# Lo parts of queries and keys on GpSimd instead of VectorE, in a fused attention, pooling and feed-forward step

## The chip, the cores and the metric

The kernel runs on one core of a Trainium2 chip. The metric is device time in microseconds (us); the median of three runs before the change is 1396.32 us (1395.48 to 1396.6).

## The reference, cut to what matters

One transformer layer, in fp32, for a prompt of 1024 rows and for 8 decoding samples with 4096 cached rows each. The part around the change is the prompt's attention: 8 heads of 64 columns, causal, with a bias from summed log forget gates.

```python
def fox_prompt(q, k, v, logf):
    Fh = jnp.cumsum(logf, axis=1).transpose(0, 2, 1)
    ...
    s = einsum('bqhd,bkhd->bhqk', q_blk, k) * HEAD_DIM ** -0.5
    s = s + (F_blk[..., :, None] - Fh[..., None, :])
    s = where(kpos <= qpos, s, NEG_INF)
    p = softmax(s, axis=-1)
    return einsum('bhqk,bkhd->bqhd', p, v)
```

The rest of the layer: projections of prompt and samples, a pooling mixer, attention of the samples over their cached pages, the output product, two layer norms and a gated feed-forward product.

## The kernel before, in words

**Hi and lo parts.** A product in full fp32 is made as a sum of matmuls in a faster rounded type (fp32r). Each operand x is split into a hi part (x rounded, a copy, made by ScalarE) and a lo part (x - hi, a subtraction). For a weight tile the hi part is in `WH`, the lo part in `WL`; for the prompt's rows they are `XH` and `XL`. For the queries and keys of a pair of heads both parts of both heads lie in `R2`: six tiles of 128x1024, three per head. Tile 3*hh has the query (hi in the head's own 64 partitions, lo in the other 64), tiles 3*hh+1 and 3*hh+2 the key's hi part twice and its lo part twice, so that two matmuls of 128 contraction rows make all four terms. The raw query is in `QX` (ACC tile 6), the raw key in `KX[p % 2]` (ACC tiles 7 and 4).

**Slots.** The prompt's attention runs over four pairs of heads (p = 0 to 3) with 16 slots each (s = 0 to 15; slots 0 to 7 are head 0, 8 to 15 head 1); x = 16 * p + s counts them all, 64 in sum. Slot x makes one tile of 128 query rows against up to 1024 keys. In each slot the engines do this, each in an order written out by hand:

- TensorE: scores of x (L1264 and L1268, into `S`, PSUM banks 0 and 1), extra turns (transposes) in some slots, a first half of product steps, the turn of the probabilities of x-1 (L1218, into `TB`, PSUM banks 4 and 5), a second half of product steps, then the weighted values of x-2 (L1278, into `OB`). The product steps (L1205, three matmuls each) are shares of the projections for the next pair, dealt over the slots beforehand (`CHUNKS`): in slot 1 of a pair three and three for pairs 0 to 2, four and three for pair 3.
- VectorE: bias and row minimum of the scores (L1748), then what else the slot has, then the copy of turned probabilities out of `TB` for even x-1 (L1791), a reciprocal (L1795), and the scaling of the weighted values of x-2 (L1809).
- ScalarE: exponentials (L989), the copies of finished projections out of PSUM (`keep`, L892 to L895), the copy of turned probabilities for odd x-1 (L1008), hi parts.

`TB` is one tile that all turns share, in a fixed order (`T`). In slot 1 of every pair TensorE turns the raw values of that pair into `TB` right after the scores (L1218 again), VectorE copies them to `VN[p % 2]` (L1783), and only then may TensorE write the turn of the probabilities of the slot before into `TB` (`claim_tb` waits for `tb_free`).

**The lo parts of queries and keys** are made by VectorE, one instruction of 64x1024 each, counted by the semaphore `conv_lo`: `query_lo(p, hh)` (L1631) and `key_lo(p, hh, n)` (L1637, n = 0 and 1). Those of head 0 of pair p+1 come in slots 11 (query), 12 and 13 (keys); those of head 1 of pair p in slot 0 (query) and slot 1 (both keys), in each slot right behind L1748 and ahead of everything else, and so ahead of L1783 in slot 1. Those of pair 0 are made before slot 0. ScalarE makes the hi parts just ahead (`query_hi` L902 in slots 10 and 15, `key_hi` L909 in slots 11, 12 and 0; semaphore `conv_hi`). Who waits for `conv_lo`: the scores of the first tile of a head (slots 0 and 8), `keep` before it overwrites the raw query or key tile, and GpSimd at its pauses.

**GpSimd in these slots** subtracts the lo parts of later weight tiles (`entry_rest`, L778, ten in all, among them at slots 10, 16, 21, 26, 32, 37, 42 and 48) and multiplies pages of cached keys by the first two samples' queries (`multiply`, L769, 32 of them, two pages or 128x1024 each). The multiplications are spread over the slots of `EMUL`, none of them in slots 0, 1, 11, 12 or 13 of a pair:

```python
ESLOTS = [x for x in range(8, 48) if x % STEPS not in (0, 1, 11, 12, 13)]
EMUL = tuple(ESLOTS[n * len(ESLOTS) // EARLY] for n in range(EARLY))
ERED = tuple(x + 1 for x in EMUL)
```

VectorE reduces each product one slot later (`reduce_keys`, L1654, slots `ERED`), and SP loads the next pages behind the reductions. GpSimd isn't tied to the slots but by what it waits for; the two waits for `conv_lo` (its pauses), at s = 2 of pairs 1 and 2 and at s = 14 of pairs 0 and 1, keep its next multiplications behind VectorE's subtractions.

**Behind the prompt** come the mixer and the samples' projections (from about 320 us), the output product with the first layer norm (from about 400 us), and then the feed-forward product, into which the samples' attention over cached pages is woven.

Of the kernel before, what the change touches and what calls it, by code (L numbers as in the profile page):

```python
# [24 lines left out]
F32 = mybir.dt.float32  # L25
# [3 lines left out]
ALU = mybir.AluOpType  # L29
# [5 lines left out]
KC = D // P  # L35
# [6 lines left out]
PAIRS = H // 2  # L42
# [20 lines left out]
NWT = 3 * PAIRS + GROUPS  # L63
WS = 3
# [30 lines left out]
ENTRY = {n + WS: x for n, x in LASTSLOT.items() if n + WS < NWT}  # L95
# [43 lines left out]
EMUL = tuple(ESLOTS[n * len(ESLOTS) // EARLY] for n in range(EARLY))  # L139
# [71 lines left out]
def build(nc, t):  # L211
    ctx = ExitStack()
    with ctx:  # L213
# [520 lines left out]
        def _(pool):  # L734
# [21 lines left out]
            def multiply(n):  # L756
# [9 lines left out]
                if c == 0:  # L766
# [2 lines left out]
                pool.tensor_tensor(keys, keys, QB[:].rearrange("p (o n) -> p o n", o=1).to_broadcast([P, KP, AW]),  # L769
                                   ALU.mult).then_inc(k_mul, 1)  # L770

            def entry_rest(n):

                e = KC + n
                pool.wait_ge(ent_hi, e + 1)
                pool.wait_ge(ent_lo, e)
                hi, lo = WH[:, tile_slot(n), :], WL[:, tile_slot(n), :]
                pool.tensor_tensor(lo, WR[:, raw_slot(e), :], hi.bitcast(F32), ALU.subtract).then_inc(ent_lo, 1)  # L778

            for x, p, s in slots():  # L780
                if x == 6:
                    pool.wait_ge(tb_free, T["g", 1] + 1)
                    for b in range(NB):
                        pool.dma_start(G_d[b], GT[:, b // 4, (b % 4) * NPAGE * H:(b % 4 + 1) * NPAGE * H]).then_inc(g_st, 16)
                if s == 2 and 1 <= p < PAIRS - 1:
                    pool.wait_ge(conv_lo, 6 * p + 6)
                if s == 14 and p + 1 < PAIRS - 1:
                    pool.wait_ge(conv_lo, 6 * (p + 1) + 3)
                for n in range(2 * WS, NWT):
                    if ENTRY[n] + 1 == x:  # L790
                        entry_rest(n)
                for n in range(EARLY):
                    if EMUL[n] == x:
                        multiply(n)
# [821 lines left out]
        def _(dve):  # L1616
# [8 lines left out]
                    hi, lo = (part[:, max(0, e - 1), 0:ROWS] for part in (XH, XL))  # L1625
                dve.tensor_tensor(lo, WR[:, raw_slot(e), :], hi.bitcast(F32), ALU.subtract).then_inc(ent_lo, 1)  # L1626

            def query_lo(p, hh):
                a, b = slice(64 * hh, 64 * hh + 64), slice(64 - 64 * hh, 128 - 64 * hh)
                dve.wait_ge(conv_hi, 6 * p + 3 * hh + 1)  # L1630
                dve.tensor_tensor(R2[b, 3 * hh, :], QX[a, :], R2[a, 3 * hh, :].bitcast(F32), ALU.subtract  # L1631
                                  ).then_inc(conv_lo, 1)

            def key_lo(p, hh, n):
                a, b = slice(64 * hh, 64 * hh + 64), slice(64 - 64 * hh, 128 - 64 * hh)
                dve.wait_ge(conv_hi, 6 * p + 3 * hh + 2)
                dve.tensor_tensor(R2[(a, b)[n], 3 * hh + 2, :], KX[p % 2][a, :], R2[a, 3 * hh + 1, :].bitcast(F32),  # L1637
                                  ALU.subtract).then_inc(conv_lo, 1)

            def reduce_keys(n):  # L1640
# [73 lines left out]
            dve.scalar_tensor_tensor(out=fa, in0=fz, scalar=-1.0, in1=fz, op0=ALU.mult, op1=ALU.max).then_inc(f_z, 1)  # L1714
            dve.wait_ge(f_t, 1)
            dve.tensor_scalar(fnf, fb, 1.0, None, ALU.add).then_inc(f_u, 1)
            query_lo(0, 0)
            dve.wait_ge(f_l, 1)
            link(dve.tensor_scalar(fnf, fnf, -1.0, None, ALU.add))
            link(dve.tensor_tensor(fnf, fb, fnf, ALU.subtract))  # L1720
# [3 lines left out]
            dve.wait_ge(f_done, 1)  # L1724
            link(dve.tensor_tensor_scan(fnf[:, 0:ROWS], fone, fz[:, 0:ROWS], 0.0, ALU.mult, ALU.subtract))
            dve.tensor_scalar(fnf[:, 0:ROWS], fnf[:, 0:ROWS], 1.0 / SCALE, None, ALU.mult).then_inc(f_done, 1)
            key_lo(0, 0, 0)
            key_lo(0, 0, 1)
            dve.wait_ge(ob_full, O["ft"] + 1)
            dve.wait_ge(small_lo, 2)  # L1730
            link(dve.tensor_copy(f_rows.rearrange("p i h -> p (i h)"), OB[:, 0:RT * H]))
            dve.tensor_copy(f_new[:], OB[0:NB, RT * H:(RT + 1) * H]).then_inc(ob_free, 1)
            query_lo(0, 1)
            key_lo(0, 1, 0)
            key_lo(0, 1, 1)
            for n in range(WS):
                entry_lo(KC + WS + n)

            for x, p, s in slots():
                if x < SLOTS:  # L1740
                    hh, i = s // RT, s % RT
                    w = (i + 1) * P
                    dve.wait_ge(s_full, U["s", x] + 1)
                    if i == 0:
                        dve.wait_ge(nf_ld[hh], 16 * (p + 1))
                    if x >= 2:
                        dve.wait_ge(tb_full, T["t", x - 2] + 1)
                    dve.tensor_tensor_reduce(L[x % 2][:, 0:w], S[:, 0:w], NF[hh][:, 0:w], -SCALE, 3e38,  # L1748
                                             ALU.add, ALU.min, negm[:, x % 2:x % 2 + 1]).then_inc(s_free, 1)
                if s == 11 and p + 1 < PAIRS:  # L1750
                    query_lo(p + 1, 0)
                if s in (12, 13) and p + 1 < PAIRS:
                    key_lo(p + 1, 0, s - 12)
                if s == 0 and 1 <= p < PAIRS:
                    query_lo(p, 1)
                if s == 1 and 1 <= p < PAIRS:
                    key_lo(p, 1, 0)
                    key_lo(p, 1, 1)
                for n in range(EARLY):
                    if ERED[n] == x and EMUL.index(EMUL[n]) == n:  # L1760
                        reduce_keys(n)
                if x in (3, 5):
                    m = (x - 3) // 2
                    dve.wait_ge(ob_full, O["q", m] + 1)
                    dve.tensor_copy(QB[0:NB, 2 * m * P:(2 * m + 2) * P], OB[0:NB, 0:2 * P]).then_inc(ob_free, 1)
                if x == 2:
                    dve.wait_ge(suf_scan, 2)
                    dve.wait_ge(ob_full, O["c"] + 1)
                    for m in range(2):
                        ls = LS[:, m, :].rearrange("p (h k) -> p h k", h=H)  # L1770
                        tot = OB[:, m * H:(m + 1) * H].rearrange("p (h o) -> p h o", o=1).to_broadcast([P, H, P])
                        ins = dve.tensor_tensor(ls, tot, ls, ALU.subtract)
                    ins.then_inc(ob_free, 1)
                if x in (4, 5):
                    m = x - 4
                    dve.wait_ge(tb_full, T["g", m] + 1)
                    dve.tensor_copy(GT[:, m, :].rearrange("p (r h) -> p r h", h=H),
                                    TB.rearrange("p (h r) -> p r h", h=H)).then_inc(tb_free, 1)
                if s == 1 and p < PAIRS:
                    dve.wait_ge(tb_full, T["vn", p] + 1)  # L1780
                    if p >= 2:
                        dve.wait_ge(vn_st, 16 * (p - 1))
                    dve.tensor_copy(VN[p % 2], TB).then_inc(tb_free, 1)  # L1783
                v = x - 1
                if 0 <= v < SLOTS:
                    if v % 2 == 0:
                        w = (v % RT + 1) * P
                        dve.wait_ge(tb_full, T["t", v] + 1)
                        if v >= 2:
                            dve.wait_ge(ob_full, O["pv", v - 2] + 1)  # L1790
                        dve.tensor_copy(PT[0][:, 0:w], TB[:, 0:w]).then_inc(tb_free, 1)  # L1791
                    dve.wait_ge(e_done, v + 1)
                    if v >= 2:
                        dve.wait_ge(ob_free, O["pv", v - 2] + 1)
                    dve.reciprocal(rinv[:, v % 2:v % 2 + 1], rsum[:, v % 2:v % 2 + 1]).then_inc(inv_done, 1)  # L1795
                for n in range(EARLY):
                    if ERED[n] == x and EMUL.index(EMUL[n]) != n:
                        reduce_keys(n)
                if x in MIXSLOT:
                    mixer_output(MIXSLOT[x])  # L1800
                v = x - 2
                if v >= 0:
                    q, r = divmod(v, STEPS)
                    hh, i = r // RT, r % RT
                    dve.wait_ge(ob_full, O["pv", v] + 1)
                    dve.wait_ge(inv_done, v + 1)
                    if r == 0 and q >= 1:
                        dve.wait_ge(tb_full, T["ct", q - 1] + 1)
                    dve.tensor_scalar(AO[:, i * P + hh * HD:i * P + hh * HD + HD], OB[:, 0:HD],  # L1809
                                      rinv[:, v % 2:v % 2 + 1], None, ALU.mult).then_inc(ob_free, 1)  # L1810
                if x < 2:
                    dve.wait_ge(logf_ld, 32)
                    dve.wait_ge(mask_done, 1)
                    link(dve.tensor_tensor_scan(LS[:, x, :], scanmask, LF[:, x, :], 0.0, ALU.mult, ALU.add))
                    dve.tensor_copy(suftot[:, x, :], LS[:, x, :].rearrange("p (h k) -> p h k", h=H)[:, :, P - 1]
                                    ).then_inc(suf_scan, 1)
                if x + 1 in MIXSLOT:
                    mixer_input(MIXSLOT[x + 1])
                if x == SLOTS - 2:
                    output_lo(0)  # L1820
# [451 lines left out]
```

## Time and profile before

| | us |
|---|---|
| median of three runs | 1396.32 |
| the profiled execution's own time | 1396.35 |
| its span, first to last instruction | 1394.5 |
| TensorE matmuls busy | 1343.7 (96%) |
| TensorE weight loads busy | 1078.8 (77%) |
| VectorE busy | 693.9 (50%) |
| ScalarE busy | 358.6 (26%) |
| GpSimd busy | 548.5 (39%) |
| mean granted TensorE clock | 0.989 |

How to read it: the engines run beside each other, each through its own list of instructions in order, and wait for each other by semaphores. Busy times add up over the whole span and say nothing of where an engine waits; the list of waits and the timeline do. PE is TensorE's matmuls, PEld its weight loads, DVE is VectorE, ACT ScalarE, POOL GpSimd. A granted clock of 1.00 is 2.4 GHz and of 0.5 is 1.2 GHz. Names left of the arrow are written, names right of it read; `AR` and `ACC` are large tiles of which `VN`, `L`, `PT`, `QX` and `KX` are parts, and R stands for `R2`.

### The profile page before, as it was taken

The numbers are of one execution on the slowest core, as the hardware profiler recorded it, in microseconds if no ns is written. First come the engines' busy times: TensorE is split into PE (matmuls) and PEld (weight loads), VectorE is DVE, ScalarE is ACT, GpSimd is POOL, SyncE is SP. The second block draws the span as 40 slices with busy tenths as digits, with TensorE's granted clock in tenths as the row PEclk, the third lists the DMA queues.
The fourth block names the chain that finished last, engine by engine and source line by source line (L and its number), as shares of the span: only waits on it lengthen the run. The fifth ranks groups of instructions, "written<-read, shape, count | busy, mean of one in ns | idle before, by whom it ended". The sixth has DMA issues, their size and how long they took to land. (4 is left out here: it accounts for less than half of the span.)

```text
span 1394.5 us, 21289 instructions
## 1 busy us (share of the span) xinstructions
PE 1343.7 (96%) x7605; PEld 1078.8 (77%) x7605; DVE 693.9 (50%) x1038; ACT 358.6 (26%) x527; POOL 548.5 (39%) x262
## 2 busy tenths in 40 slices
PE   7899999999989899999999999999999999999997
PEld 5889999999869886677777777777777776666675
DVE  4745665653556583553546465544634334321327
ACT  3524444443341233112021202121210201111116
POOL 1014454704110036656575657566562212121114
PEclk9999999999989999999999999999999999999999
DMA  7334453511035216777777777778776445367533
GB/s 246 104 116 150 129 185 103 170 43 53 25 107 219 86 45 220 256 243 243 231 261 240 243 247 241 234 236 266 222 253 215 158 141 202 152 262 277 223 145 122
DMA packets 111769, 255.02 MB, mean 183 GB/s; under 512 B 12848, under 2 KB 22961, under 8 KB 106280
## 3 DMA queue, kind: packets, MB, share of 16 engines
q1 hardware_dynamic: 102384, 247.00, 53.0%
q10 hardware_dynamic: 8320, 4.19, 1.1%
q0 software_dynamic: 960, 2.47, 0.5%
q8 instruction: 60, 0.98, 0.3%
q14 instruction: 45, 0.37, 0.1%
HBM read 243.73 MB, written 10.12 MB: 182 GB/s over the span
## 5 line engine op out<-in xcount | busy, mean ns | idle before, releaser
L829 POOL TENSOR_TENSOR WL<-WR,WH 128x1024 fp32r<-128x1024 f32 x55 | 132.1, 2402 | 427.4 <-ACT WH L1051 427.4
L769 POOL TENSOR_TENSOR AR<-AR,QB 128x1024 f32<-128x1024 f32 x96 | 232.6, 2439 | 101.1 <-DMA AR<-cache_k 88.5
L1454 PE MATMUL PSM<-XH,WH 128*128 128x512 f32 x672 | 215.7, 402 | 0.0
L1454 PE MATMUL PSM<-XL,WH 128*128 128x512 f32 x672 | 210.7, 395 | 0.0
L1454 PE MATMUL PSM<-XH,WL 128*128 128x512 f32 x672 | 210.7, 394 | 0.0
L2029 DVE TENSOR_TENSOR ACC<-ACC,PSM 128x512 f32<-128x512 f32 x160 | 108.7, 684 | 141.6 <-PE PSM L1464 141.5
L1454 PEld LDWEIGHTS PSM<-XH,WH 128*128 128x128 f32 x672 | 121.9, 188 | 53.3 <-issue 27.6
L1051 ACT CAST WH<-WR 128x1024 fp32r<-128x1024 f32 x55 | 57.5, 1047 | 367.3 <-PE PSM L1454 189.5
L1454 PEld LDWEIGHTS PSM<-XH,WL 128*128 128x128 f32 x672 | 126.3, 188 | 29.9
L1454 PEld LDWEIGHTS PSM<-XL,WH 128*128 128x128 f32 x672 | 126.2, 188 | 29.6
L1464 PE MATMUL PSM<-R 128*128 128x512 f32 x528 | 148.5, 390 | 0.1
L1654 DVE TENSOR_REDUCE AR<-AR 128x16 f32<-128x1024 f32 x80 | 96.8, 1211 | 91.5 <-POOL AR L769 91.5
L1464 PE MATMUL PSM<-WH,R 128*128 128x512 f32 x352 | 140.6, 400 | 0.1
L1205 PE MATMUL PSM<-XH,WH 128*128 128x344 f32 x384 | 134.2, 350 | 5.7 <-DVE WL L1626 4.7
L1205 PE MATMUL PSM<-XH,WL 128*128 128x344 f32 x384 | 123.7, 322 | 0.0
L1205 PE MATMUL PSM<-XL,WH 128*128 128x344 f32 x384 | 123.5, 322 | 0.0
L1464 PEld LDWEIGHTS PSM<-R 128*128 128x128 f32 x528 | 99.0, 188 | 22.1 <-DVE R L2017 0.5
L989 ACT ACTIVATE AR<-AR,negm 128x128 f32<-128x128 f32 (+3 forms) x64 | 49.7, 777 | 157.0 <-DVE negm L1748 157.0
L1464 PEld LDWEIGHTS PSM<-WH,R 128*128 128x128 f32 x352 | 66.1, 188 | 29.3 <-issue 12.8
L1205 PEld LDWEIGHTS PSM<-XH,WH 128*128 128x128 f32 x384 | 73.4, 191 | 8.8 <-DVE WL L1626 5.5
L2010 DVE TENSOR_TENSOR AR<-AR,PSM 128x1024 f32<-128x1024 f32 x21 | 25.6, 1220 | 107.9 <-PE PSM L1454 102.0
L1205 PEld LDWEIGHTS PSM<-XL,WH 128*128 128x128 f32 x384 | 73.4, 191 | 0.7 <-issue 0.7
(266 smaller groups left out, 2144.3 us busy)
## 6 DMA issues: line engine op xcount, KB each, us to landing
AR<-cache_v SPq DMA_DIRECT2D x256, 256.0 KB, 3.3
AR<-cache_k SPq DMA_DIRECT2D x192, 256.0 KB, 3.5
AR<-ws SPq DMA_DIRECT2D x37, 1024.0 KB, 6.4
WR<-ffn SPq DMA_DIRECT2D x66, 512.0 KB, 4.8
WR<-w_in SPq DMA_DIRECT2D x20, 512.0 KB, 4.7
ACC<-cache_k SPq DMA_DIRECT2D x32, 256.0 KB, 3.0
WR<-cache_k SPq DMA_DIRECT2D x32, 256.0 KB, 3.0
WR<-w_o SPq DMA_DIRECT2D x5, 1024.0 KB, 4.9
```

The lines of the kernel that those rows point to most:

```text
L769: pool.tensor_tensor(keys, keys, QB[:].rearrange("p (o n) -> p o n", o=1).to_broadcast([P, KP, AW]), ALU.mult).then_inc(k_mul, 1)
L829: pool.tensor_tensor(lo, WR[:, raw_weight(e), :], hi.bitcast(F32), ALU.subtract).then_inc(ffn_lo, 1)
L989: act.activation(L[x % 2][:, 0:w], L[x % 2][:, 0:w], ACT.Exp, scale=-1.0, bias=negm[:, x % 2:x % 2 + 1], accum_out=rsum[:, x % 2:x % 2 + 1 ...
L1051: act.copy(weight_slot(kind, f)[0], WR[:, raw_weight(e), :]).then_inc(ffn_hi, 1)
L1205: ins = pe.matmul(third(n, m), w[a][:, tile_slot(n), k * P:(k + 1) * P], x[b][:, k, m * TH:(m + 1) * TH], start=(k == 0 and (a, b) == PART ...
L1454: ins = pe.matmul(out[:, hc], (hi, lo)[a][:, k * P:(k + 1) * P], x[b][:, k, hc], start=(k == 0 and n == 0), stop=(k == KC - 1 and n == 2))
L1464: ins = pe.matmul(PSM[:, 2 + n % 4, :], R2[:, 2 * r + a, i * P:(i + 1) * P], w[b][:, half * HALF:(half + 1) * HALF], start=(r == 0 and m = ...
L1654: dve.tensor_reduce(out[:, c * KP:(c + 1) * KP, :].rearrange("p j h -> p (j h)"), keys.rearrange("p (a n) -> p a n", n=HD), AX.X, ALU.add) ...
L2010: dve.tensor_tensor(GU, GU, PSM[:, 2:4, :].rearrange("p a n -> p (a n)"), ALU.mult).then_inc(gu_done, 1)
L2029: dve.tensor_tensor(cols, cols, PSM[:, 2 + n % 4, :], ALU.add).then_inc(d_free, 1)
```

## The change

The lo parts of pairs 1 to 3 are made by GpSimd, in the same slots as before (11, 12, 13, 0 and 1), each behind a wait for `conv_hi` and followed by a wait for its own `conv_lo`. Ahead of each group GpSimd waits until its own multiplications (`k_mul`) and weight subtractions (`ent_lo`) of earlier slots have finished. The two pauses at s = 2 and s = 14 are gone. In slots with an `entry_rest` (16, 32, 48) the query's subtraction stands ahead of it. Pair 0's lo parts stay on VectorE, at the same places.

```diff
@@ gpsimd
+            def query_lo(p, hh):
+                a, b = slice(64 * hh, 64 * hh + 64), slice(64 - 64 * hh, 128 - 64 * hh)
+                pool.wait_ge(conv_hi, 6 * p + 3 * hh + 1)
+                pool.tensor_tensor(R2[b, 3 * hh, :], QX[a, :], R2[a, 3 * hh, :].bitcast(F32), ALU.subtract
+                                  ).then_inc(conv_lo, 1)
+                pool.wait_ge(conv_lo, 6 * p + 3 * hh + 1)
+
+            def key_lo(p, hh, n):
+                a, b = slice(64 * hh, 64 * hh + 64), slice(64 - 64 * hh, 128 - 64 * hh)
+                pool.wait_ge(conv_hi, 6 * p + 3 * hh + 2)
+                pool.tensor_tensor(R2[(a, b)[n], 3 * hh + 2, :], KX[p % 2][a, :], R2[a, 3 * hh + 1, :].bitcast(F32),
+                                  ALU.subtract).then_inc(conv_lo, 1)
+                pool.wait_ge(conv_lo, 6 * p + 3 * hh + 2 + n)
...
-                if s == 2 and 1 <= p < PAIRS - 1:
-                    pool.wait_ge(conv_lo, 6 * p + 6)
-                if s == 14 and p + 1 < PAIRS - 1:
-                    pool.wait_ge(conv_lo, 6 * (p + 1) + 3)
+                if s in (0, 1) and 1 <= p < PAIRS or s in (11, 12, 13) and p + 1 < PAIRS:
+                    pool.wait_ge(k_mul, sum(at < x for at in EMUL))
+                    pool.wait_ge(ent_lo, KC + 2 * WS + sum(ENTRY[n] + 1 < x for n in range(2 * WS, NWT)))
+                if s == 11 and p + 1 < PAIRS:
+                    query_lo(p + 1, 0)
+                if s in (12, 13) and p + 1 < PAIRS:
+                    key_lo(p + 1, 0, s - 12)
+                if s == 0 and 1 <= p < PAIRS:
+                    query_lo(p, 1)
+                if s == 1 and 1 <= p < PAIRS:
+                    key_lo(p, 1, 0)
+                    key_lo(p, 1, 1)
                 for n in range(2 * WS, NWT):
                     if ENTRY[n] + 1 == x:
                         entry_rest(n)
@@ vector
-            def query_lo(p, hh):
+            def first_query_lo(hh):
...
-            def key_lo(p, hh, n):
+            def first_key_lo(hh, n):
...
-                if s == 11 and p + 1 < PAIRS:
-                    query_lo(p + 1, 0)
-                if s in (12, 13) and p + 1 < PAIRS:
-                    key_lo(p + 1, 0, s - 12)
-                if s == 0 and 1 <= p < PAIRS:
-                    query_lo(p, 1)
-                if s == 1 and 1 <= p < PAIRS:
-                    key_lo(p, 1, 0)
-                    key_lo(p, 1, 1)
```

`first_query_lo` and `first_key_lo` are the old functions for pair 0 alone.

## Rows read from the trace of the kernel before

**Rows 1.** The page's busy line: busy us (share of the span) xinstructions.

```profile
PE 1343.7 (96%) x7605; PEld 1078.8 (77%) x7605; DVE 693.9 (50%) x1038; ACT 358.6 (26%) x527; POOL 548.5 (39%) x262
```

**Rows 2.** Waits of TensorE, 95 to 320 us: total us, times, longest us.

```profile
PE PSM L1218 <- DVE AR L1783: 3.3, 2, 1.9
...
PE PSM L1218 <- DVE ACC L1783: 1.9, 1, 1.9
```

**Rows 3.** Timeline of TensorE, slots 17 and 49: start us, us, instruction, [idle before].

```profile
148.91 1.05 PE L1218 MATMUL PSM<-ident_sb,AR 128*128 128x128 f32 x8
...
151.06 0.31 PE L1205 MATMUL PSM<-XH,WL 128*128 128x344 f32 x1
153.24 0.33 PE L1218 MATMUL PSM<-ident_sb,AR 128*128 128x128 f32 x1 [1.87 <-DVE AR L1783]
...
299.46 1.05 PE L1218 MATMUL PSM<-ident_sb,AR 128*128 128x128 f32 x8
...
303.79 0.33 PE L1218 MATMUL PSM<-ident_sb,AR 128*128 128x128 f32 x1 [1.40 <-DVE AR L1783]
```

**Rows 4.** Timeline of VectorE, slots 17 and 19.

```profile
149.58 2.47 DVE L1637 TENSOR_TENSOR R<-ACC,R 64x1024 fp32r<-64x1024 f32 x2
151.98 1.21 DVE L1783 COPY AR<-PSM 128x1024 f32<-128x1024 f32 x1
...
164.39 1.20 DVE L1654 TENSOR_REDUCE PR<-WR 128x16 f32<-128x1024 f32 x1
```

**Rows 5.** Timeline, slot 1 (pair 0), TensorE and VectorE.

```profile
67.25 1.06 PE L1218 MATMUL PSM<-ident_sb,AR 128*128 128x128 f32 x8
...
68.35 1.23 DVE L1783 COPY ACC<-PSM 128x1024 f32<-128x1024 f32 x1 [0.47 <-PE PSM L1218]
...
69.42 0.31 PE L1205 MATMUL PSM<-XH,WL 128*128 128x344 f32 x1
...
69.63 0.33 PE L1218 MATMUL PSM<-ident_sb,AR 128*128 128x128 f32 x1
```

**Rows 6.** Groups of VectorE by line, 95 to 320 us: busy us, mean ns, idle before.

```profile
L1637 DVE TENSOR_TENSOR R<-ACC,R 64x1024 fp32r<-64x1024 f32 x12 | 14.6, 1219 | 0.3
...
L1631 DVE TENSOR_TENSOR R<-ACC,R 64x1024 fp32r<-64x1024 f32 x6 | 10.3, 1725 | 0.2
```

**Rows 7.** Timelines of VectorE and of GpSimd, slot 43.

```profile
271.94 3.35 DVE L1631 TENSOR_TENSOR R<-ACC,R 64x1024 fp32r<-64x1024 f32 x1
...
271.85 5.71 POOL L769 TENSOR_TENSOR WR<-WR,QB 128x1024 f32<-128x1024 f32 x2
```

**Rows 8.** Groups of GpSimd by line, 100 to 480 us.

```profile
L769 POOL TENSOR_TENSOR WR<-WR,QB 128x1024 f32<-128x1024 f32 x16 | 39.0, 2449 | 10.0 <-DVE R L1637 9.7 <-DMA WR<-cache_k 0.4
L769 POOL TENSOR_TENSOR ACC<-ACC,QB 128x1024 f32<-128x1024 f32 x16 | 37.9, 2386 | 32.7 <-DVE R L1637 21.2 <-DMA QB<-q_d 11.2 <-DMA ACC<-cache_k 0.4
L778 POOL TENSOR_TENSOR WL<-WR,WH 128x1024 fp32r<-128x1024 f32 x9 | 22.1, 2457 | 77.7 <-ACT WH L867 77.7
L814 POOL TENSOR_TENSOR AR<-AR 128x1024 f32<-128x1024 f32 x6 | 11.8, 1975 | 0.5
```

**Rows 9.** Timelines of ScalarE and of GpSimd, slots 15 to 18.

```profile
142.55 1.04 ACT L902 CAST R<-ACC 64x1024 fp32r<-64x1024 f32 x1
...
144.75 2.55 POOL L778 TENSOR_TENSOR WL<-WR,WH 128x1024 fp32r<-128x1024 f32 x1 [6.61 <-ACT WH L867]
152.13 4.69 POOL L769 TENSOR_TENSOR WR<-WR,QB 128x1024 f32<-128x1024 f32 x2 [4.84 <-DVE R L1637]
```

**Rows 10.** Timelines of VectorE and of GpSimd, slots 22 to 24.

```profile
180.62 1.08 DVE L1791 COPY AR<-PSM 128x896 f32<-128x896 f32 x1
...
176.77 4.76 POOL L769 TENSOR_TENSOR ACC<-ACC,QB 128x1024 f32<-128x1024 f32 x2
```

**Rows 11.** Windows: us; PE, PEld, DVE, ACT, POOL busy; granted clock; DMA; GB/s.

```profile
384.00:404.00 20.00, 14.68 (x69) 9.71 (x69) 9.07 (x18) 5.58 (x10) 3.67 (x7) 0.66 0.31 111
...
520.00:530.00 10.00, 7.64 (x38) 4.25 (x37) 5.34 (x6) 3.35 (x3) 3.00 (x2) 0.83 0.34 106
```

More of the change, by code:

```diff
@@ L1626, in entry_lo @@
                 dve.tensor_tensor(lo, WR[:, raw_slot(e), :], hi.bitcast(F32), ALU.subtract).then_inc(ent_lo, 1)
-            def query_lo(p, hh):
+            def first_query_lo(hh):
                 a, b = slice(64 * hh, 64 * hh + 64), slice(64 - 64 * hh, 128 - 64 * hh)
-                dve.wait_ge(conv_hi, 6 * p + 3 * hh + 1)
+                dve.wait_ge(conv_hi, 3 * hh + 1)
                 dve.tensor_tensor(R2[b, 3 * hh, :], QX[a, :], R2[a, 3 * hh, :].bitcast(F32), ALU.subtract
                                   ).then_inc(conv_lo, 1)
-            def key_lo(p, hh, n):
+            def first_key_lo(hh, n):
                 a, b = slice(64 * hh, 64 * hh + 64), slice(64 - 64 * hh, 128 - 64 * hh)
-                dve.wait_ge(conv_hi, 6 * p + 3 * hh + 2)
-                dve.tensor_tensor(R2[(a, b)[n], 3 * hh + 2, :], KX[p % 2][a, :], R2[a, 3 * hh + 1, :].bitcast(F32),
+                dve.wait_ge(conv_hi, 3 * hh + 2)
+                dve.tensor_tensor(R2[(a, b)[n], 3 * hh + 2, :], KX[0][a, :], R2[a, 3 * hh + 1, :].bitcast(F32),
                                   ALU.subtract).then_inc(conv_lo, 1)
@@ L1716, in _ @@
             dve.tensor_scalar(fnf, fb, 1.0, None, ALU.add).then_inc(f_u, 1)
-            query_lo(0, 0)
+            first_query_lo(0)
             dve.wait_ge(f_l, 1)
@@ L1726, in _ @@
             dve.tensor_scalar(fnf[:, 0:ROWS], fnf[:, 0:ROWS], 1.0 / SCALE, None, ALU.mult).then_inc(f_done, 1)
-            key_lo(0, 0, 0)
-            key_lo(0, 0, 1)
+            first_key_lo(0, 0)
+            first_key_lo(0, 1)
             dve.wait_ge(ob_full, O["ft"] + 1)
@@ L1732, in _ @@
             dve.tensor_copy(f_new[:], OB[0:NB, RT * H:(RT + 1) * H]).then_inc(ob_free, 1)
-            query_lo(0, 1)
-            key_lo(0, 1, 0)
-            key_lo(0, 1, 1)
+            first_query_lo(1)
+            first_key_lo(1, 0)
+            first_key_lo(1, 1)
             for n in range(WS):
```

## The prediction

> **What bounds the kernel now.** I read the page's busy line first: TensorE is busy 96% of the span, VectorE 50%, GpSimd 39% [rows 1]. Taking work from VectorE can shorten the kernel only where TensorE stands still for VectorE. So the second view is the list of waits of TensorE between 95 and 320 us, the stretch in which pairs 1 to 3 of heads run. 5.2 us of it end with L1783, VectorE's copy of the turned values: two waits make 3.3 us, the longer 1.9, and a third is 1.9 [rows 2]; of the list's three other rows two are ScalarE's, and the last is 0.4 us for VectorE in pair 0. Third, the TensorE timeline where they stand: slots 17, 33 and 49, the second slot of pairs 1, 2 and 3, with waits of 1.87, 1.87 and 1.40 us. In slot 17 the last product matmul starts at 151.06 and the next instruction, a turn of probabilities, only at 153.24; slot 33 repeats it, and slot 49 goes on at 303.79 [rows 3]. Fourth, VectorE in slot 17: after the scores it runs two subtractions of keys (L1637, 2.47 us for two) and only then the copy L1783, at 151.98 for 1.21 us [rows 4]. The turn of the values had started at 148.91 [rows 3] and lain ready since about 150.0. TensorE may not write the next turn into that PSUM tile before the copy is done, so it waits.
>
> **A twin without the two subtractions** is slot 1, where pair 0's lo parts are already made. Its turn starts at 67.25, the copy at 68.35 (1.10 us later) and lasts 1.23 us, and TensorE goes from its last product matmul at 69.42 to the turn at 69.63: 0.21 us between starts [rows 5], where slot 17 shows 2.18.
>
> **The change, part by part.**
>
> 1. *Six subtractions per pair leave VectorE, in pairs 1 to 3.* That is 12 of L1637 at 1.22 us and 6 of L1631 at 1.73 on average, 25 us of VectorE [rows 6]. Nearly all of it lies beside TensorE's work and is worth nothing. What counts is slots 17, 33 and 49. In slot 17 the copy can start at 148.91 + 1.10 = 150.01, ends 1.21 us later at 151.22, and TensorE, which needs 0.21 us from start to start, arrives at 151.27. It went on at 153.24: 1.97 us won, 0.1 more than the wait that the view shows, since that counts from the modelled end of the last matmul. Slot 33 is the same with the same wait, 1.97. In slot 49 the turn starts at 299.46, so the copy would end at 301.77; TensorE has one product step more and arrives later by itself, the wait being shorter: 1.40 + 0.1 = 1.50 [rows 3]. **Sum: 1.97 + 1.97 + 1.50 = 5.4 us.**
>
> 2. *The collisions go.* One query subtraction took 3.35 us instead of 1.22, beside two multiplications on GpSimd that took 5.71 us [rows 7]; the mean of 1.73 [rows 6] says that the six lost 3.0 us in all. They stand in slots where TensorE has no wait for VectorE [rows 2], so I count nothing; the product steps cover them, and without that cover it would be 3.0 us.
>
> 3. *GpSimd gets 18 subtractions.* The trace shows none of 64 partitions on GpSimd, nor one whose output lies in other partitions than its inputs. Nearest is the same subtraction on 128x1024, L778, 2.46 us on average [rows 8]; the length along a partition is the same, so I take 2.46. From below: VectorE's 1.22 [rows 6]. From above: 5.71 - 2.39 = 3.3 us, the held-up one of the two multiplications in [rows 7], 2.39 being the mean of the undisturbed kind [rows 8]. In all 18 x 2.46 = 44 us, for an engine that between 100 and 480 us waits 77.7 us for ScalarE at L778 and 30.9 us at its pauses [rows 8].
>
> 4. *Pauses and new waits.* Removed are the waits for VectorE before the multiplications of slots 14, 18, 30 and 34, 9.7 + 21.2 us of idle time [rows 8]. In their place GpSimd waits for ScalarE's hi parts and for its own last instruction. Such a self-wait stands in L814's chain, whose six show 0.5 us of idle time together [rows 8], 0.1 us each; two or three for each of 18 subtractions are under 5 us of GpSimd, hidden like the rest.
>
> 5. *What is queued behind, and who waits.* The tightest place is slots 16 to 21. ScalarE's hi part of the query runs from 142.55 to 143.6; query_lo then to 146.2; the weight subtraction L778, which ran at 144.75, to 148.8; the keys' two to 151.3 and 153.9; the multiplications of slot 18 start at 154.0 instead of 152.13, and the second ends at 158.7 [rows 9]. VectorE reduces it in slot 19, at 164.39 [rows 4], or 162.4 once 1.97 us are won: 3.7 us of slack. ScalarE overwrites the query tile in slot 17, behind product steps that follow TensorE's turn of 148.91 [rows 3], and query_lo is done by 146.2. The scores that use the parts come seven slots on. SP's loads of pages wait for VectorE's reductions, which stay in their slots. In slots 11 to 13 GpSimd, like VectorE before, follows ScalarE's casts, so the multiplications of slots 14 and 30 start within about 1.2 us of where they did. Those of slots 46 and 47, which had run early at 271.85 [rows 7], come after slot 45's subtraction; two of 2.4 us fit into the two slots of about 4 us before VectorE asks.
>
> 6. *Does GpSimd slow the copy itself?* VectorE's copies out of PSUM ran beside GpSimd's multiplications at full rate: at 180.62, 896 columns took 1.08 us while GpSimd worked from 176.77 on for 4.76 us [rows 10]; that is the rate of the 1024 columns in 1.21 us of [rows 4], when GpSimd stood still. So I count nothing. What collided in [rows 7] was an operation with two inputs in SBUF: it ran from 271.94 to 275.29, which is the end of GpSimd's first (about 274.2) plus 1.1. The Trainium skill (SBUF — State Buffer, "SBUF: two separate sides") says that the two engines share a pair of ports as an exclusive lock, which VectorE needs in a two-port mode or with two SBUF inputs, and that the loser waits for the whole instruction. By that rule the copy, whose one input is in PSUM, is not held up; the trace agrees, and the sum by it is the same. Were every instruction of VectorE under the lock, rival B would be the outcome.
>
> **Against the clock.** The profiled execution took 1396.35 us (span 1394.5 and 1.85 around it); the median of the runs is 1396.32, the same to 0.03. Behind the prompt each step is released by TensorE's own progress, so the gain should stay: **1396.35 - 5.4 = 1390.9**. What may move it is the granted clock, 0.66 over 384 to 404 us and 0.83 over 520 to 530 [rows 11]: spells at 1.2 instead of 2.4 GHz at the changes of stage, where TensorE is busy 14.7 of 20 us. The change brings the work 5.4 us forward, and a spell can then end sooner or later against it. The second lasted (1 - 0.83) x 10 / 0.5 = 3.4 us; as much more or less of it over dense work is 1.7 us. With 0.6 us for the spread of the runs (1395.48 to 1396.6) the forecast's own range is 1388.5 to 1393.2.
>
> **Rivals.**
>
> *A. The gain is given back* at the half-rate spells or at a wait behind the prompt. For it: TensorE's work is thin at the change of stages [rows 11], and several engines release it there. Against: what feeds these waits comes 5.4 us earlier too. Both spells longer by 3.4 us gives 1394.3, all given back 1396.3. Chance 0.07.
>
> *B. Slower: GpSimd's key subtractions hold up the copy in slots 17, 33 and 49.* It decides once the copy is held over 2 us past its due time. It would start after both subtractions: in slot 17 at 153.9, ending at 155.1 instead of 153.2 (151.98 + 1.21), 1.9 us later than before; for three such slots 5.7 us: 1402.0. For it: [rows 7], where VectorE lost 2.1 us that way. Against: [rows 10], where a copy did not. Chance 0.03.
>
> *C. The subtraction costs far more on GpSimd.* The slack of 3.7 us in step 5 is reached after three subtractions, so from 2.46 + 3.7 / 3 = 3.7 us each VectorE's reductions wait for GpSimd, in pairs 1 and 2, and the turns behind them in VectorE's order come late. If all of that reached TensorE, the gain would be used up 2.7 us per pair later, at 4.6 us each: 1396.3, and beyond it slower. The upper bound of step 3 stays below the point where anything is late. Chance 0.02.
>
> *D. The copy is not what holds TensorE*, another releaser stands right behind it: 1396.3. The twin speaks against it. Chance 0.02.
>
> **The numbers.** 0.2% (2.8 us) is about what a measurement of this kernel can tell from no change; faster means below 1393.5. The forecast has 0.86, the rivals 0.14. Of A more than half lies within 0.2%, D and half of C too; B and the rest of C are slower. Faster 0.88, same 0.08, slower 0.04. The range, 1388.5 to 1394.0, takes in the forecast's own and a part of A.
>
> **What the changed profile would show.** In slots 17, 33 and 49 the copy L1783 starts right after its turn, and TensorE's wait for it is gone (step 1); the subtractions last about 2.46 us on GpSimd (step 3), and VectorE's operations beside them keep their durations (steps 2 and 6); VectorE's reductions wait under 2 us in all for GpSimd (step 5); the prompt ends 5.4 us sooner, and the end follows. I would be wrong if TensorE still waited for VectorE at L1218 in these slots, if reductions waited for GpSimd, or if the lead at 320 us had gone by the end.

## The result and the profile after

| | before | after |
|---|---|---|
| median, first comparison (5 executions each) | 1396.19 us | 1387.89 us |
| ratio, 95% interval | | 0.9942 (0.9927 to 0.9956) |
| span of the profiled execution | 1394.5 us | 1386.0 us |
| VectorE busy | 693.9 us | 662.1 us |
| GpSimd busy | 548.5 us | 591.0 us |
| mean granted TensorE clock, profiled execution | 0.989 | 0.992 |

The kernel is faster by 8.3 us or 0.58%. I had forecast 5.4 us, and the range ended at 1388.5: the direction was right, the time lies 0.6 us below the range. Two later comparisons on other executions gave medians of 1389.19 and 1389.53 us, with ratios of 0.9944 and 0.9954: both lie inside the range. The first comparison happened to be the fastest of the three. Over all three the changed kernel ran 17 times, with a mean of 1389.0 us. The comparisons made in the study hold 51 executions of the kernel before, with a mean of 1396.5. By these means the gain is 7.5 us (standard error 0.6).

The page's busy line of the kernel after, to hold against [rows 1]:

```profile
PE 1342.4 (97%) x7605; PEld 1079.1 (78%) x7605; DVE 662.1 (48%) x1020; ACT 359.0 (26%) x527; POOL 591.0 (43%) x280
```

VectorE has 18 instructions fewer and GpSimd 18 more. Of the 31.8 us that VectorE lost, 24.9 are the moved subtractions [rows 6]; the rest scatters from execution to execution (the reordered kernel below, from which nothing moved, shows 688.8). The list of TensorE's waits between 95 and 320 us, to hold against [rows 2] (total us, times, longest us):

```profile
PE PSM L1240 <- ACT AR L943: 2.2, 3, 0.7
PE PSM L1240 <- ACT ACC L952: 0.6, 2, 0.3
PE PSM L1240 <- DVE ACC L1791: 0.4, 1, 0.4
```

The three waits for the copy of the turned values are gone; the lines for ScalarE and for pair 0's copy (L1777 before, L1791 now) are those that had stood beside them. (Lines are shifted: L1218, L1783, L1205 and L1748 of before are L1240, L1797, L1227 and L1771 now.) The timeline of slot 17, TensorE, then VectorE, then GpSimd, which answers to [rows 3], [rows 4] and [rows 9]:

```profile
149.57 1.05 PE L1240 MATMUL PSM<-ident_sb,AR 128*128 128x128 f32 x8
...
151.71 0.31 PE L1227 MATMUL PSM<-XH,WL 128*128 128x344 f32 x1
151.94 0.33 PE L1240 MATMUL PSM<-ident_sb,AR 128*128 128x128 f32 x1
...
149.77 0.42 DVE L1771 CUSTOM_DVE_ANT_0 AR<-PSM,AR 128x256 f32<-128x256 f32 x1
150.12 0.08 DVE L1771 DVE_READ_ACCUMULATOR2_ANT negm<- 128x1 f32 x1
150.66 1.23 DVE L1797 COPY AR<-PSM 128x1024 f32<-128x1024 f32 x1 [0.46 <-PE PSM L1240]
...
144.41 2.39 POOL L775 TENSOR_TENSOR R<-ACC,R 64x1024 fp32r<-64x1024 f32 x1 [7.40 <-ACT R L924]
146.88 2.38 POOL L792 TENSOR_TENSOR WL<-WR,WH 128x1024 fp32r<-128x1024 f32 x1
149.39 4.83 POOL L782 TENSOR_TENSOR R<-ACC,R 64x1024 fp32r<-64x1024 f32 x2
154.31 4.71 POOL L769 TENSOR_TENSOR WR<-WR,QB 128x1024 f32<-128x1024 f32 x2
```

The copy starts 1.09 us after its turn, while GpSimd makes the keys' lo parts from 149.39 to 154.22, and takes 1.23 us, as in the twin of [rows 5]. TensorE goes from its last product matmul to the next turn in 0.23 us, where it took 2.18. The groups of GpSimd, 95 to 320 us, give the price of a moved subtraction:

```profile
L782 POOL TENSOR_TENSOR R<-ACC,R 64x1024 fp32r<-64x1024 f32 x12 | 28.6, 2384 | 6.6 <-ACT R L931 5.9
...
L775 POOL TENSOR_TENSOR R<-ACC,R 64x1024 fp32r<-64x1024 f32 x6 | 14.3, 2382 | 22.4 <-ACT R L924 22.2
```

**Where the time went, instruction by instruction.** I laid the two traces side by side and took, for the same instruction, its start after minus its start before (my subtraction of timeline rows). The lead grows by 1.96 us at slot 17, 1.97 at slot 33 and 1.62 at slot 49: 5.55 us. Before slot 2 the profiled execution after is 0.65 us *behind*. Between 385 and 404 us it wins 1.9 us, where a half-rate spell of the clock (a stretch at 1.2 instead of 2.4 GHz) is shorter: granted clock 0.91 over 376 to 412 us, 0.81 before. At 759 us one wait of TensorE for VectorE (1.0 us before) is missing, 1.1 us. That wait comes and goes: another profile of the changed kernel has it (1.0 us), and two of the four further profiles of the kernel before that are shown below have not. The rest of the span brings 0.7. Together -0.65 + 5.55 + 1.9 + 1.1 + 0.7 = 8.6, the 8.5 by which the spans differ. So the slots did what the forecast said, and 3 us came from elsewhere in this pair of executions. The experiments ask whether they are part of the change.

### The profile page after: what moved, and what is told of

Same layout as the page of the kernel before. It is cut to its first block and busy times, and to the rows that moved or that the text cites. A ratio compares the mean times of both kernels' runs of the same rounds, so it can differ in the third digit from the quotient of the medians.

```text
span 1386.0 us, 21314 instructions
## 1 busy us (share of the span) xinstructions
PE 1342.4 (97%) x7605; PEld 1079.1 (78%) x7605; DVE 662.1 (48%) x1020; ACT 359.0 (26%) x527; POOL 591.0 (43%) x280
## 3 DMA queue, kind: packets, MB, share of 16 engines
q0 software_dynamic: 960, 2.47, 0.5%
## 5 line engine op out<-in xcount | busy, mean ns | idle before, releaser
L1227 PE MATMUL PSM<-XH,WH 128*128 128x344 f32 x384 | 134.7, 351 | 5.0 <-DVE WL L1648 5.0
L1227 PE MATMUL PSM<-XH,WL 128*128 128x344 f32 x384 | 123.9, 323 | 0.0
L1227 PE MATMUL PSM<-XL,WH 128*128 128x344 f32 x384 | 123.8, 322 | 0.0
L1227 PEld LDWEIGHTS PSM<-XH,WH 128*128 128x128 f32 x384 | 73.7, 192 | 7.9 <-DVE WL L1648 5.8
L1227 PEld LDWEIGHTS PSM<-XL,WH 128*128 128x128 f32 x384 | 73.9, 192 | 0.7 <-issue 0.7
```

Source lines behind the costliest of these rows:

```text
L1227: ins = pe.matmul(third(n, m), w[a][:, tile_slot(n), k * P:(k + 1) * P], x[b][:, k, m * TH:(m + 1) * TH], start=(k == 0 and (a, b) == PART ...
```

## The experiments

Of each kernel I give the time and, from its profile, the stretches between the starts of VectorE's row minimum (L1748 or its later line) of slots 16 and 20 and of slots 32 and 36. Before: 22.56 and 22.57 us. After: 20.59 and 20.60.

### The copy first, nothing on GpSimd

```diff
-                if s == 1 and 1 <= p < PAIRS:
+                if s == 1 and 1 <= p < PAIRS and p not in (1, 2, 3):
                     key_lo(p, 1, 0)
                     key_lo(p, 1, 1)
...
                     dve.reciprocal(rinv[:, v % 2:v % 2 + 1], rsum[:, v % 2:v % 2 + 1]).then_inc(inv_done, 1)
+                if s == 1 and p in (1, 2, 3):
+                    key_lo(p, 1, 0)
+                    key_lo(p, 1, 1)
```

The edit is made to the kernel before. Two more kernels do the same for slot 17 alone (p in (1,)) and for slots 17 and 33 (p in (1, 2)).

> The kernel before with one change: in slots 17, 33 and 49 VectorE makes the copy of the turned values and that of the probabilities first and the two key subtractions behind them; nothing moves to GpSimd. Theory 1 (the copy held up by the two subtractions is all that the change mends): the three waits of TensorE for L1783 vanish, 5.5 us are won inside the slots, and the total comes out like the changed kernel's, 1386 to 1391. Rival (the relief of VectorE, 25 us, or the missing collisions are worth the part of the gain above 5.5 us): the total stays at 1390.9 or above. Rival 2 (GpSimd is what brings the gain): 1396.

> The same reordering in slot 17 alone: 2.0 us won in the slots. If gain simply adds up, 1394.3. If what was won beyond the 5.5 us comes from half-rate spells of TensorE's clock that lie differently against the work once it comes earlier, the total may differ from 1394.3 by some 1.7 to 3.4 us either way, and the profile shows other spells around the change of stage near 390 us.

> The same reordering in slots 17 and 33: 4.0 us won in the slots. Adding up: 1392.3. With the clock theory again up to 3.4 us off that, with the spells near 390 us shorter or longer than the 13.7 us of before.

| copy first in | won in the slots, by the traces | median | ratio, 95% interval |
|---|---|---|---|
| slot 17 | 1.97 | 1395.08 (12 executions) | 0.9990 (0.9979 to 1.0002) |
| slots 17, 33 | 3.96 | 1392.09 (6) | 0.9965 (0.9952 to 0.9977) |
| slots 17, 33, 49 | 5.55 | 1390.30 (6) | 0.9951 (0.9936 to 0.9966) |

The total of the first row isn't clear of noise by itself. Its profile also shows what comes back below: a half-rate spell behind the wait that was left in slot 33, whose stretch took 24.11 us instead of 22.57, so that slots 2 to 63 together won only 0.4 us there.

VectorE's timeline of slot 17 with the copy first:

```profile
151.25 1.23 DVE L1783 COPY AR<-PSM 128x1024 f32<-128x1024 f32 x1 [0.46 <-PE PSM L1218]
152.90 0.29 DVE L1791 COPY AR<-PSM 128x128 f32<-128x128 f32 x1 [0.42 <-PE PSM L1218]
153.10 0.15 DVE L1795 RECIPROCAL rinv<-rsum 128x1 f32<-128x1 f32 x1
153.29 2.47 DVE L1637 TENSOR_TENSOR R<-ACC,R 64x1024 fp32r<-64x1024 f32 x2
```

With the copy first in all three, the stretches of the slots come out as in the changed kernel to 0.03 us (slots 2 to 63 take 301.58 us in both), without one instruction on another engine. What wins time in the slots is the order at L1783.

### The moved subtractions without slot 1's keys

The changed kernel, with the two `key_lo` of slots 17, 33 and 49 back on VectorE ahead of the copy; the semaphore's order is kept by two waits.

```diff
@@ gpsimd, changed kernel
                 if s == 11 and p + 1 < PAIRS:
+                    pool.wait_ge(conv_lo, 6 * p + 6)
                     query_lo(p + 1, 0)
...
-                if s == 1 and 1 <= p < PAIRS:
-                    key_lo(p, 1, 0)
-                    key_lo(p, 1, 1)
@@ vector, behind L1748
+                if s == 1 and 1 <= p < PAIRS:
+                    dve.wait_ge(conv_lo, 6 * p + 4)
+                    key_lo(p, 1, 0)
+                    key_lo(p, 1, 1)
```

> The changed kernel, but the two key subtractions of slots 17, 33 and 49 stay on VectorE ahead of the copy, as before; the other twelve are GpSimd's and the pauses are gone. Theory 1: TensorE's three waits for the copy are back, and the total is that of before, 1396 (within 0.2%). Rival (relief of VectorE and missing collisions count): 1393 or less.

It took 1408.47 us (6 executions), ratio 1.0090 (1.0076 to 1.0104): neither theory's figure. Two rows of its timelines, slot 17, and one of TensorE's waits between 95 and 320 us show why:

```profile
149.21 5.92 DVE L1664 TENSOR_TENSOR R<-ACC,R 64x1024 fp32r<-64x1024 f32 x2
...
148.36 5.69 POOL L769 TENSOR_TENSOR WR<-WR,QB 128x1024 f32<-128x1024 f32 x2
...
PE PSM L1238 <- DVE AR L1805: 6.7, 2, 5.3
```

I had left GpSimd's pause out with the rest, so its multiplications of slot 18 ran into VectorE's two subtractions, which took 5.92 us instead of 2.47. Two runs take this apart. One is the kernel before with nothing but the pauses removed:

```diff
-                if s == 2 and 1 <= p < PAIRS - 1:
-                    pool.wait_ge(conv_lo, 6 * p + 6)
-                if s == 14 and p + 1 < PAIRS - 1:
-                    pool.wait_ge(conv_lo, 6 * (p + 1) + 3)
```

> The kernel before with GpSimd's four pauses removed and all lo parts left on VectorE. Theory 1 (the multiplications of slots 18 and 34 then run beside VectorE's two key subtractions, each of which waits for a whole multiplication): the two subtractions take about 5.9 us instead of 2.47 in slots 17 and 33, TensorE's waits for the copy grow from 1.9 to about 5.3 us there, and the total is 7 us or more above before, up to 1408 if the clock falls to half rate in those waits. Rival (the pauses cost nothing and are worth nothing): 1396.

1410.13 us (4 executions), ratio 1.0098 (1.0078 to 1.0118). VectorE's two subtractions of slot 17 against GpSimd's multiplications, and TensorE's waits:

```profile
149.12 6.75 DVE L1633 TENSOR_TENSOR R<-ACC,R 64x1024 fp32r<-64x1024 f32 x2
...
146.80 4.71 POOL L769 TENSOR_TENSOR WR<-WR,QB 128x1024 f32<-128x1024 f32 x2
151.45 6.64 POOL L769 TENSOR_TENSOR ACC<-ACC,QB 128x1024 f32<-128x1024 f32 x2
...
PE PSM L1214 <- DVE AR L1779: 7.5, 2, 6.1
PE PSM L1214 <- DVE ACC L1779: 6.1, 1, 6.1
```

The waits for the copy are 13.6 us instead of 5.2 and the whole is 14 us slower, so the pauses, far from costing anything, held off collisions. By the waits it is the pauses at slots 18 and 34 that count; TensorE's list has nothing new for those at slots 14 and 30. The other 5 us are half-rate spells behind the waits of 6.1 us (granted clock 0.77 over 150 to 165 us and 0.78 over 225 to 245). GpSimd's second pair of multiplications lost too, 6.64 us instead of 4.71. The Trainium skill (SBUF — State Buffer, "SBUF: two separate sides") says that the one who loses the shared ports waits for the other's whole instruction; the 4.3 us that two subtractions lost here, against GpSimd's 2.4 for one multiplication, agree with it.

The other run is the kernel with the keys left, with the pause of s = 2 put back. It ran in two comparisons:

```diff
+                if s == 2 and 1 <= p < PAIRS - 1:
+                    pool.wait_ge(conv_lo, 6 * p + 6)
```

> The run that left slot 17's, 33's and 49's key subtractions on VectorE, now with the pauses ahead of the multiplications of slots 18 and 34 put back. Theory 1: the subtractions take 2.47 us for two again, TensorE's waits for the copy are 1.9, 1.9 and 1.4 us as before the change, and the total is 1396 within 0.2%, though 12 of 18 subtractions are GpSimd's: moving them is worth nothing. Rival (the moved twelve are worth something): 1393 or less; or (they cost something, as the 1408 of that run might suggest): over 1399.

> Twelve subtractions on GpSimd, the keys of slots 17, 33 and 49 ahead of the copy on VectorE, two pauses kept, once more. Its mechanism is that of before: mean 1395 to 1397. Its clock was 0.9913 over ten executions, like the changed kernel's, with none of the time won; if that stays, the clock isn't kept up by the missing waits, and if it goes to 0.9895 as before, it was chance.

1395.96 us (10 executions; ratio 0.9998, 0.9986 to 1.0011) and 1396.98 (12; 0.9996, 0.9984 to 1.0008). The six subtractions left on VectorE between 95 and 320 us, at full rate again:

```profile
L1666 DVE TENSOR_TENSOR R<-ACC,R 64x1024 fp32r<-64x1024 f32 x6 | 7.3, 1222 | 0.2
```

With twelve of 18 subtractions on GpSimd, the collisions of slots 11 and 43 gone and VectorE relieved by 17.6 us, nothing is won. All of the gain comes from taking the six key subtractions of slots 17, 33 and 49 from ahead of the copy.

### The two kernels again

> The changed kernel once more, beside the reordered one and the kernel before. The first comparison gave 8.3 us where the slots give 5.5. Theory 1 (5.5 us of mechanism, and the rest is where the half-rate spells of TensorE's clock fall, by chance from execution to execution): the median lies near 1390.5, between 1388.5 and 1391.5, and the profile shows spells of other length or place than the first. Rival (the relief of VectorE or the missing collisions win 2.5 us somewhere): the median lies near 1388 again, 2 us or more below the reordered kernel's.

> The reordered kernel (copy first in slots 17, 33 and 49, nothing on GpSimd) once more, as the partner of the changed kernel on the same chip. Theory 1: the same time as the changed kernel within 1.5 us. Rival: 2 us or more above it.

> The changed kernel a third time, beside the three below. Over two comparisons it stood 7.8 us under before on the mean of 11 executions, with a mean clock of 0.9916 against 0.9895, where the slots give 5.5. Theory (5.5 us of mechanism, and the rest is less time at half rate): mean 1387 to 1391, and clock and time go together from execution to execution. If the extra 2 us are chance, this mean comes nearer to 1390.7 and the clock nearer to 0.990; if something in the change keeps the clock up, both stay.

> The reordered kernel a third time. Same time as the changed kernel within 1.5 us by the theory that the copy's wait is all; 2 us above it if the relief of VectorE counts.

| | median, each comparison | mean of all | mean clock of all |
|---|---|---|---|
| before | 1395.97, 1396.20, 1397.27 | 1396.5 (51 executions) | 0.9895 |
| changed | 1387.89, 1389.19, 1389.53 | 1389.0 (17) | 0.9916 |
| copy first, three slots | 1390.30, 1388.05, 1390.69 | 1389.5 (17) | 0.9915 |
| keys stay, pause kept | 1395.96, 1396.98 | 1396.3 (22) | 0.9906 |

The changed kernel and the reordered one can't be told apart (0.5 us, with standard errors of 0.6 each), so the relief of VectorE isn't what wins more than the slots hold. Both win 7 to 7.5 us where the slots hold 5.55, and both have a higher mean clock. A line fitted through all executions of the study, with one level per kernel and the half-rate time taken from the mean clock, gives 0.33 us of time (standard error 0.03) for each us spent at half rate; at equal clock the changed kernel is 5.6 us under before (0.5) and the reordered one 5.2. So the extra goes with half-rate time. That is a correlation and no more: the same fit puts the kernel with the keys left 0.8 us (0.4) above the one before, for which no mechanism is known.

### Where the extra comes from: four more profiles of the kernel before

In TensorE's timelines of the profiles with the waits, the wait was sometimes followed by matmuls at half rate. Four more profiles of the kernel before, without any edit, add eight places.

> The kernel before, looked at again. In the profiles so far the stretch of slots 16 to 20 (and 32 to 36) takes 20.6 us without TensorE's wait of 1.9 us and 22.6 with it, but in two of seven cases with the wait a half-rate spell of 3.4 or 6.8 us follows it and the stretch takes 24.1 or 25.3. Theory (the waits sometimes pull the clock down, which is the part of the gain above 5.5 us): over four looks, eight such places, one to four have a spell, and the others are at 22.6. Rival (the two were chance of another kind, and the extra 2 us lie elsewhere): none of eight.

> As the look before it: each of slots 16 to 20 and 32 to 36 at 22.6 us, or 24 to 25.4 us with a half-rate spell behind the wait.

> As the look before it: each of slots 16 to 20 and 32 to 36 at 22.6 us, or 24 to 25.4 us with a half-rate spell behind the wait.

> As the look before it: each of slots 16 to 20 and 32 to 36 at 22.6 us, or 24 to 25.4 us with a half-rate spell behind the wait.

| kernel before, profile | slots 16 to 20 | slots 32 to 36 | whole, us |
|---|---|---|---|
| first | 22.56 | 22.56 | 1398.56 |
| second | 25.21 | 22.57 | 1398.82 |
| third | 22.55 | 22.56 | 1396.08 |
| fourth | 25.22 | 22.53 | 1397.60 |

TensorE in slots 17 and 18 of the first of these profiles:

```profile
153.15 0.33 PE L1218 MATMUL PSM<-ident_sb,AR 128*128 128x128 f32 x1 [1.87 <-DVE AR L1783]
...
154.73 1.89 PE L1278 MATMUL PSM<-ACC,AR 128*128 128x64 f32 x16
```

and of the second, with the window's row (us; PE, PEld, DVE, ACT, POOL busy; granted clock; DMA share; GB/s):

```profile
153.22 0.33 PE L1218 MATMUL PSM<-ident_sb,AR 128*128 128x128 f32 x1 [1.87 <-DVE AR L1783]
...
154.95 3.51 PE L1278 MATMUL PSM<-ACC,AR 128*128 128x64 f32 x16
158.22 0.99 PE L1264 MATMUL PSM<-R 128*128 128x384 f32 x2
...
150.00:165.00 15.00, 13.13 (x71) 12.56 (x70) 5.04 (x11) 3.15 (x8) 9.34 (x4) 0.77 0.08 30
```

The same 1.87 us of waiting; then 16 matmuls take 1.89 us once and 3.51 the other time. The changed kernel's row for this window:

```profile
150.00:165.00 15.00, 14.71 (x104) 13.86 (x103) 6.93 (x18) 4.29 (x10) 13.55 (x6) 1.00 0.29 79
```

Over all 16 profiles, leaving out the two kernels whose waits were made longer: of 15 places with a wait of 1.87 us (slots 17 and 33), four had a spell behind it and took 1.5 to 2.8 us more; of 17 places without the wait, none. In the seven profiles with both waits the spells cost 2.76 + 2.65 + 2.69 us, 1.2 us on average. By this average, itself of only three spells in seven profiles, that is most of the 1.9 us between 7.5 and 5.55; the other 0.7 is no more than the means' uncertainty. The two kernels with waits of 5.3 to 6.1 us had a spell in all four such places.

Which executions get the spell can be told beforehand. The windows around the first slots of the first and second profile (columns as above):

```profile
55.00:75.00 20.00, 14.77 (x88) 14.12 (x88) 16.59 (x23) 7.42 (x14) 1.46 (x2) 0.83 0.37 110
...
55.00:75.00 20.00, 14.77 (x96) 13.97 (x95) 16.52 (x23) 7.35 (x14) 1.46 (x2) 0.91 0.38 110
```

All four profiles with a spell behind a wait of 1.87 us have 0.91 there, and the four that have such waits and no spell have 0.83. Three profiles of kernels without these waits have 0.91 too and show no spell in the slots. In these profiles it took both, the wait and an execution of that kind; what makes the kind isn't shown. The spells at the change of stage don't explain the extra: over 376 to 412 us the granted clock is 0.88 on average in the seven profiles with both waits and 0.86 in the six of the changed and the reordered kernel.

### A version that uses the room

In slot 11 TensorE waited 0.7 us for ScalarE's copy of the turned keys. VectorE, free of the query subtraction there, makes it, and TensorE takes one product step more ahead of its next turn.

```diff
+    for p in range(PAIRS - 1):
+        c = 2 * 11
+        chunks[p, c], chunks[p, c + 1] = chunks[p, c] + chunks[p, c + 1][:1], chunks[p, c + 1][1:]
...
@@ scalar, slot 11
-                    key_rows(p + 1)
+                    store_rows("kn", p + 1)
@@ vector, behind L1748
+                if s == 11 and p + 1 < PAIRS:
+                    dve.wait_ge(tb_full, T["kn", p + 1] + 1)
+                    dve.wait_ge(kn_st, 16 * (p + 1))
+                    dve.tensor_copy(KN, TB).then_inc(tb_free, 1)
```

> A version that uses the room on VectorE: the changed kernel, and in slot 11 of pairs 0 to 2 VectorE instead of ScalarE copies the turned keys out of PSUM, and TensorE does one product step more ahead of the next turn there (3 and 1 instead of 2 and 2). TensorE waited 0.7 us for ScalarE's copy at each of the three. Expected: these waits go, the slots win 2 us more than the changed kernel's 5.5, and the total is 1386 to 1388. Rival: the later copy of probabilities on VectorE makes a new wait in slot 12, and nothing is won.

1388.10 us (5 executions), ratio to before 0.9941 (0.9925 to 0.9957). All of TensorE's waits from 95 to 320 us:

```profile
PE PSM L1243 <- ACT ACC L955: 0.6, 2, 0.3
```

Slots 2 to 63 take 299.11 us against 301.58 of the changed kernel: 2.5 us are won there. In the whole it stood 1.4 us under the changed kernel's median of the same comparison (1389.53), less than these five and six executions can tell, with a mean clock that happened to be lower (0.9902). In the slots it beats both kernels, in total it beats the one before, and its lead over the changed kernel isn't established.

## Why the prediction was right or wrong

**What bounds the kernel, and step 1, were right to about a tenth.** Slots 17, 33 and 49 were forecast at 1.97 + 1.97 + 1.50 and gave 1.96 + 1.97 + 1.62. The last was low because TensorE, arriving behind the copy, needs only 0.15 us from start to start there (298.80 to 298.95), and the turn after it is a little shorter too. The twin in slot 1 gave the copy's due time and the floor of the gap exactly. This was no luck: in three profiles of the changed kernel slots 2 to 63 agree to 0.01 us. That nothing but the order at L1783 counts was argued from the list of waits and is now shown, from both sides: the copy first without the move wins all, the move without these keys wins nothing.

**Step 2** (collisions count nothing) holds: in the kernel with the keys left they are gone and nothing was won. **Step 3**: 2.38 us per subtraction against 2.46 assumed; half the partitions and a shift to the other half change nothing. **Step 5**: slot 18's multiplications start at 154.31, 0.65 us of it the late start of this execution, against 154.0 forecast. VectorE's waits for GpSimd were to be under 2 us and are 3.2, against 1.4 before; all four lie in slots 9 to 11 of pair 0, where no moved subtraction stands ahead of the multiplication. The largest, 1.33 us, is the query subtraction's old collision turned into a wait for the same multiplication, and TensorE doesn't feel it. **Step 6** and rival B: the copy beside GpSimd's subtractions took 1.23 us; B didn't happen.

**Step 4 was half told.** I priced the pauses as idle time of GpSimd and nothing else. Those at slots 18 and 34 are worth 14 us in the kernel before, as the run without the pauses shows. The change may drop them only because it takes away VectorE's instruction that they protect; it was right to drop both together, and my text didn't say so.

**The step that failed is the clock's, in the part "Against the clock".** I saw half-rate spells only at the changes of stage, gave them 1.7 us either way around a mean of nothing, and set the range's lower end by that (1390.9 - 1.7 - 0.6 is 1388.6; I wrote 1388.5). Two things were wrong. A wait of 1.9 us amid dense work is itself sometimes followed by a spell, and the profile before happened to show none; ending the waits ends these spells too, a gain of 1.2 us on average, and only a gain. The sum had nothing for it. And the spells move a single execution by more than I allowed: executions of the kernel before run from 1390.5 to 1402.6 us in the study, against the 1395.48 to 1396.6 of the three shown, from which I took 0.6 us. With 5.55 + 1.2 in the middle and 2.5 us either way the range would have held 1387.89. That the first comparison fell below my range, and the two later ones into it, is chance of this second kind. **Rival A** didn't happen: the gain was kept behind the prompt, and the spells in the slots added to it instead of taking from it. **C** and **D** are excluded by the timeline.

What isn't settled: whether the 0.7 us left is anything, what decides which executions get a spell behind the short wait, and why twelve moved subtractions with the waits in place show a mean clock of 0.9906 against 0.9895 without gaining time.

## What to carry to other kernels

When the bounding engine waits for a shared buffer, look first at what its releaser does just before the release: putting the copy ahead of two unhurried instructions won the same here, to within the error, as moving them to another engine. A pause whose purpose isn't visible in the waits may be holding two engines' two-input operations apart, so remove it only together with what it protects. Price a removed wait of TensorE at its length and somewhat more, since its clock may drop behind it, and take the spread from many executions rather than from three.

## What I had not expected of the hardware

- The same wait of 1.87 us is followed in four of 15 places by matmuls at half rate (16 of them in 3.51 us instead of 1.89), for 1.5 to 2.8 us more; waits of 5.3 and 6.1 us were followed by it in four of four. The four of the 15 are in just those profiles whose granted clock over 55 to 75 us was 0.91 and not 0.83.
- Spells at the change of stage near 390 us differ from execution to execution of one kernel: granted clock 0.80 over 376 to 396 us in the kernel before, 1.00 in one profile of the kernel with keys left, whose start-to-start distances show 3.6 us less there.
- VectorE's two-input subtractions lost more than GpSimd's one multiplication when a queue of multiplications stood ready: two of them took 6.75 us instead of 2.47, each held up in turn.
